# Two attention stages of a two-layer transformer kernel: projection work placed between the head pairs, and query products merged two heads at a time

## What is computed

```python
# layer 0
proj = h @ w_in                      # c_q (256), c_kv (128), k_r (32), qB, kB, vB (512 each)
qA = (_rmsnorm(c_q, g_q) @ w_uq).reshape(B_, S, MLA_HEADS, MLA_QK)     # 8 heads of 64 + 32
q_nope, q_rope = qA[..., :MLA_NOPE], qA[..., MLA_NOPE:]
q_rope = _rope(q_rope, cos[None, :, None, :], sin[None, :, None, :])
kv = (_rmsnorm(c_kv, g_kv) @ w_ukv).reshape(B_, S, MLA_HEADS, MLA_NOPE + MLA_V)
oA = _mla_causal_attention(...)      # softmax over all earlier tokens, 8 heads
oB = _dilated_attention(qB, kB, vB, dil_slopes)   # 8 heads, three dilation patterns
return jnp.concatenate([oA, oB], axis=-1) @ w_out
# layer 1
qkv = h @ w_qkv                      # 16 query heads, 2 key/value heads of 64
return _swa_sink_attention(q, k, v, sinks, swa_slopes) @ w_out
```

## Time and profile before

| what | us |
|---|---|
| median of three runs | 1615.84 |
| the profiled execution, as timed | 1617.18 |
| its span, first to last instruction | 1615.2 |
| PE busy (matmuls) | 1432.0 |
| DVE busy | 682.2 |
| ACT busy | 540.5 |
| layer 0: from the first spread transposes to the end of e_out | 959.0 to 1106.8 |
| layer 1: the same to the end of o_out | 1309.2 to 1411.0 |
| the two feed-forward parts | 1117 to 1305, 1419.5 to the end |

### The profile page before, as it was taken

How to read it: one execution, slowest core, us unless ns; L and a number is a source line. 1 busy time by engine, 2 the same in 40 slices (tenths; PEclk the granted TensorE clock), 3 DMA queues, 4 the chain that set the end, 5 groups by cost and what they waited for, 6 DMA issues and landing times.

```text
span 1615.2 us, 25662 instructions
## 1 busy us (share of the span) xinstructions
PE 1432.0 (89%) x10764; PEld 1149.9 (71%) x10764; DVE 682.2 (42%) x1035; ACT 540.5 (33%) x853; POOL 46.8 (3%) x53
## 2 busy tenths in 40 slices
PE   6999998999779888888898869868999987899997
PEld 6989997878655444444454449557999986689997
DVE  4434786635631101101111044575555547565554
ACT  2453675144320100101001034445334345453333
POOL 0000000400020000000000000000000000000000
PEclk8987999989969999999999989969999998999999
DMA  7531442112348999999999983203545622155520
GB/s 289 186 128 53 163 166 90 55 53 92 142 196 346 428 428 429 428 428 428 428 428 428 429 365 131 79 1 133 201 176 192 226 88 79 61 187 195 181 92 27
DMA packets 27434, 349.54 MB, mean 216 GB/s; under 512 B 3041, under 2 KB 3297, under 8 KB 4578
## 3 DMA queue, kind: packets, MB, share of 16 engines
q1 hardware_dynamic: 27218, 347.46, 53.8%
q10 hardware_dynamic: 144, 1.05, 0.2%
HBM read 347.45 MB, written 1.05 MB: 216 GB/s over the span
## 4 chain that ended last, share of the span: by engine, by line
PE 69%; DMA 15%; DVE 9%; ACT 4%; issue 2%; SPq 1%; POOL 0%; DVEq 0%; POOLq 0%; ACTq 0%
PE psum L410 67%; DMA ring<-in_w 14%; ACT pages L1055 2%; DVE slot_lo L1587 2%; PE psum L479 1%; DVE pages L2068 1%; DVE pages L1722 1%; ACT mix_hi L1084 1%; DVE pages L2100 1%; DVE pages L2072 0%; DMA ab<-in_w_ab 0%; DVE pages L1548 0%; PE psum L763 0%; ACT pages L1310 0%; DVE pages L2155 0%
## 5 line engine op out<-in xcount | busy, mean ns | idle before, releaser
L410 PE MATMUL psum<-ring,pages 128*64 128x256 f32 (+1 forms) x2564 | 359.7, 438 | 67.4 <-DMA ring<-in_w 48.7
L410 PEld LDWEIGHTS psum<-ring,pages 128*64 128x64 f32 x2564 | 186.5, 142 | 225.6 <-issue 80.2
L410 PE MATMUL psum<-x_hi,gu_hi 128*128 128x256 f32 x704 | 199.9, 284 | 3.4 <-DVE x_lo L1574 3.4
L410 PE MATMUL psum<-x_hi,gu_lo 128*128 128x256 f32 x704 | 199.9, 284 | 0.0
L410 PE MATMUL psum<-x_lo,gu_hi 128*128 128x256 f32 x704 | 199.9, 284 | 0.0
L410 PE MATMUL psum<-pages 64*64 64x64 f32 (+10 forms) x1760 | 145.6, 275 | 20.4 <-ACT pages L1055 10.2
L410 PE MATMUL psum<-h_hi,mix_hi 128*128 128x256 f32 x512 | 149.0, 291 | 1.1 <-DVE slot_lo L1587 1.1
L410 PEld LDWEIGHTS psum<-pages 64*64 64x64 f32 (+4 forms) x1760 | 115.3, 161 | 48.4 <-issue 24.1
L410 PE MATMUL psum<-h_lo,mix_hi 128*128 128x256 f32 x512 | 147.3, 288 | 0.0
L410 PE MATMUL psum<-h_hi,slot_lo 128*128 128x256 f32 x512 | 147.2, 287 | 0.0
L1587 DVE TENSOR_TENSOR slot_lo<-ring,mix_hi 128x2048 fp32r<-128x2048 f32 x44 | 101.8, 2317 | 101.5 <-ACT mix_hi L1084 101.2
(11 more groups left out here) (222 smaller groups left out, 2154.0 us busy)
## 6 DMA issues: line engine op xcount, KB each, us to landing
ring<-in_w SPq DMA_DIRECT2D x96, 2048.0 KB, 18.1
ring<-in_ffn SPq DMA_DIRECT2D x44, 1536.0 KB, 6.5
ring<-in_w_in SPq DMA_DIRECT2D x16, 2048.0 KB, 8.1
ring<-in_e_in SPq DMA_DIRECT2D x3, 2048.0 KB, 14.4
ring<-in_w_pa SPq DMA_DIRECT2D x2, 2048.0 KB, 8.1
ring<-in_w_pb SPq DMA_DIRECT2D x2, 2048.0 KB, 8.7
ring<-in_w_o SPq DMA_DIRECT2D x2, 2048.0 KB, 7.7
ring<-in_e_out SPq DMA_DIRECT2D x2, 2048.0 KB, 15.0
```

What stands on the lines that cost most here:

```text
L410: return pe.matmul(o, lhsT, rhs, start=start, stop=stop, skip_group_check=True)
```

## The change

The two sections of layer 0 become one run of `attend` over eight pairs of heads (four mla, then four dil). `attend` now calls a function `fill(i)` on PE behind the scores of pair i+1, and a function `between(i)` on ACT (behind the exponentials of pair i) and on DVE (at the end of step i). Those hold half units of projections and their cutting. In layer 0 the units qB1, kB1, vB0, vB1 (half in each of steps 0 to 7) and the first half item of e_out (steps 8 and 9) move into `attend`; qB0 and kB0 stay ahead of it. vB is now made in units like the others. In layer 1 the key and value projection comes first, then unit qS0; qS1 stands whole in step 0, qS2 in steps 1 and 2, qS3 in steps 3 and 4, and the first half item of o_out in steps 8 and 9. Scores use banks 0 and 1 only, fills banks 2 and 3. Scores and values issue the two heads of a pair alternately. Weight columns of each head's latent query are laid out as 64 + 32 + 32 swapped, so that one product of 128 columns makes all of them and two heads share a bank: 16 logical matmuls in place of 32, and half as many, twice as wide instructions on ACT and DVE behind them. The ring item o_kv is loaded ahead of o_in.

```diff
-            def attend(sec, nheads, operands, values):
...
+            def attend(heads, fill, scores_need, values_need):
+
+                def scores(j):
+                    sec, n, operands, _ = heads[j]
+                    if j in scores_need:
+                        pe.wait_ge(*V(*scores_need[j]))
+                    o = [take(f"{sec}s{2 * n + h2}", h2) for h2 in range(2)]
+                    for qs, width in ((slice(0, P), P), (slice(P, T), T)):
+                        for h2 in range(2):
...
                 scores(0)
+                for i in range(len(heads) + 2):
+                    if i + 1 < len(heads):
                         scores(i + 1)
+                    fill(i)
                     if i >= 2:
...
-            for hd in range(HEADS):
-                name = f"qA{hd}"
+            for n in range(HEADS // 2):
+                name = f"qA{n}"
                 o = take(name)
-                for k in range(2):
-                    mm(o[0:NOPE + ROPE, 0:T], wq[:, k, hd * 96:(hd + 1) * 96], cq[:, k, :], k == 0, k == 1)
...
+                for half in range(2):
+                    for k in range(2):
+                        hd = 2 * n + half
+                        last = mm(o[:, half * T:(half + 1) * T], wq[:, k, hd * P:(hd + 1) * P], cq[:, k, :], k == 0, k == 1)
...
+            def late_fill(i):
+
+                if i == 0:
+                    split_unit("qS1", ("o_in", 0), 1, page_high[3], x, bank=2)
+                elif i < 3:
+                    split_unit("qS2", ("o_in", 1), 0, page_high[4], x, (i - 1,), 3)
+                elif i < 5:
+                    split_unit("qS3", ("o_in", 1), 1, page_high[3], x, (i - 3,), 2)
+                elif i >= 8:
+                    tokens_half("o_out", 0, ("o_out", 0), 0, page_high[4], y, split_ready(4), blocks=(i - 8,), banks=(2, 3))
+
             pe.wait_ge(*V("kvS_ready", 2))
+            attend(heads, late_fill, {2 * n: ("qS_ready", n + 1) for n in range(4)}, {})
...
+            def late_between(i):
+
+                if i == 0:
+                    split_high(MIXER_PAIRS + 16)
+                    queries_out(1)
+                elif i == 1:
+                    split_high(MIXER_PAIRS + 17)
+                elif i == 3:
+                    queries_out(2)
+                    split_high(MIXER_PAIRS + 18)
+                elif i == 5:
+                    queries_out(3)
+                    split_high(MIXER_PAIRS + 19)
+                elif i in (6, 7):
+                    input_high(page_part[9], fm(12), late, blocks=(i - 6,))
...
+            def late_lows(i):
+
+                for at, upto in ((0, 16), (1, 17), (3, 18), (5, 19)):
+                    if i == at:
+                        split_low(MIXER_PAIRS + upto)
```

More of the change, by code:

```diff
@@ L420, in project_split @@
                     for pair in range(2):
[L421 to L432, removed]
@@ new lines, in project_tokens, with value_unit @@
+                        tokens_half(part, i, item, c, highs[c], x, ready, width)
+            def value_unit(name, item, c, high, x, blocks, bank):
+                if 0 in blocks:
+                    split_chunk(item, c, high, (name,))
+                    take(name, bank)
+                o = bank_of(name)
+                w = {"hi": high.rearrange("p (k c) -> p k c", c=256), "lo": chunk_of(slot_low[slot_no(item_no[item])], c)}
+                for b in blocks:
+                    for k in range(KD):
+                        for n, (wp, xp) in enumerate(PARTS):
+                            last = mm(o[:, b * T:(b + 1) * T], x[xp][:, k, b * P:(b + 1) * P], w[wp][:, k, :],
+                                      k == 0 and n == 0, k == KD - 1 and n == 2)
+                if 1 in blocks:
+                    give(last, name)
+                    if c:
+                        release(item, name)
@@ L866, in attend @@
                         pe.wait_ge(*V(f"{sec}_pT", n + 1))
[L867 to L874 removed]
+                        o = take(f"{sec}o{n}", 6 + j % 2)
@@ new lines, in _, with early_fill @@
+            dil = (lambda i: (qB[half_of(i), i // 2, :], kB[half_of(i), i // 2, :]), lambda g, b: vB[:, b, g * VDIM:(g + 1) * VDIM])
+            heads = [("mla", n) + mla for n in range(HEADS // 2)] + [("dil", n) + dil for n in range(HEADS // 2)]
+            y = {"hi": page_part[3], "lo": page_part[2]}
+            def early_fill(i):
+                if i < 2:
+                    split_unit("qB1", ("e_in", 1), 1, page_high[11], x, (i % 2,), 2)
+                elif i < 4:
+                    split_unit("kB1", ("e_in", 2), 1, page_high[12], x, (i % 2,), 3)
+                elif i < 6:
+                    value_unit("vB0", ("e_in", 3), 0, page_high[11], x, (i % 2,), 2)
+                elif i < 8:
+                    value_unit("vB1", ("e_in", 3), 1, page_high[12], x, (i % 2,), 3)
+                else:
+                    tokens_half("e_out", 0, ("e_out", 0), 0, page_high[11], y, split_ready(3), blocks=(i % 2,), banks=(2, 3))
@@ L2101, in attend @@
                                                 ALU.mult), f"{sec}_probs" if b else None)
-                for n in range(pairs - 2, pairs):
-                    output(sec, n)
+                    between(i)
+                for j in range(len(heads) - 2, len(heads)):
+                    output(*heads[j][0:2])
             def output(sec, n):
```

390 lines of the change are left out of this document (218 added, 172 removed).

## The result

The changed kernel takes 1605.82 us (median of 13; 1598.59 to 1609.37 without one disturbed run) against 1615.84: ratio 0.9931, 95% interval 0.9917 to 0.9945. Its profiled execution took 1604.6 (span 1602.8, clock 0.949). The forecast was 1604.5.

The account below looks back on a forecast made before the run. Attention was taken as bound by DVE's 4.1 us per pair and the chain across engines, with PE idle beside it. Layer 0 -22.2, layer 1 +1.2 and clock +9.6 sum to -11.4: 1604.5 us against 1615.8, range 1592 to 1613.

Parts of the forecast that it names:

- Ahead of layer 0's attention: Projections before layer 0's attention: units moved away 22.7 and latent products 9.6, less 0.8, make 31.5 us less; start at 999.8.
- Layer 0's attention: Layer 0's merged attention: 51 us of PE work plus 16 us of waits, 67.0; layer 0 gains 22.2 at full clock.
- Layer 1: Layer 1: attention takes 67.6 us instead of 42.2, o_out ends at 1412.2 instead of 1411.0, a loss of 1.2.
- the sources of the waits: Layer 0's attention: 16 us from two score banks, DVE's cuts waiting for ACT's copy, and the last steps (2 us).
- the two banks: Layer 0's attention: scores of the next pair wait until DVE empties the same two banks; before there were four.
- The clock: Both attentions: half clock behind eight waits of 2.5 to 4.1 us costs 1.2 us each, 9.6 in all.
- clock holds: Rival for both attentions: dense fills keep full clock, -21.0 us and up to 2 more, 1594; chance 0.17.
- Small items: Head alternation, mode switches and DMA: alternation could bring 2 us, switches move the sum under 2, DMA 0 to 2.
- changed feed-forward parts: Sign of error, outside the mixers: the prediction is wrong if the feed-forward parts change; no size given.
- full cover: Rival: fill covers all waits and PE is the bound, attentions of 51 and 45.5 us, total 1557; chance 0.03.
- Half clock right through: Rival for both layers: half clock stays, PE blocks 1.3 times as long, +7 us together, 1623; chance 0.10.
- the slower rope: Rival in layer 0's latent queries: DVE's rope takes 2.5 per pair instead of 2.1, 1.6 us lost; no separate chance.

Follow-up runs that it names:

- experiment 7: Changed kernel with useless identity matmuls put into PE's longest waits in both attentions: 1599.89 us, ratio 0.9914.
- experiment 1: Changed kernel with layer 1 put back (all query units ahead of attention, no fill, scores over four banks), layer 0 as changed: 1593.34 us, ratio 0.9865.
- experiments 3 to 6: Changed kernel with helpers moved: 3 two query evacuations (1595.83 us); 4 ACT's and DVE's (1569.62); 5 only DVE's (1591.91); 6 as 4, layer 0 only ACT's (1573.28).
- 9: Kernel before the change with one edit, scores on banks 0 and 1 only instead of four: 1611.78 us, ratio 0.9981.
- the reordered kernel: Changed kernel with ACT's and DVE's cuts and evacuations placed elsewhere in both layers, PE untouched: 1569.62 us, ratio 0.9705; run again 1567.92 us, 0.9721.
- experiment 10: The changed kernel itself, unedited, profiled and run once more: 1607.98 us (1595.51 to 1610.22).
- with more fill: Kernel with ACT's and DVE's helpers reordered, plus output projection half items earlier and more of them in layer 1's attention: 1563.62 us, ratio 0.9686.
- experiment 8: Changed kernel with the two heads of a pair issued one behind the other in scores and values, not alternately: 1602.56 us, ratio 0.9928.

## Why the prediction was right, step by step

The mechanism was right: an interleaved attention bound by the order of helpers on ACT and DVE, a gain in layer 0 and a loss in layer 1. That the total came within 1.3 us is in part luck. The two mixers were to bring -11.4 us and brought -8.6; stages that the prediction left alone brought another -3.8, of which -4.3 is no effect of the change.

- **Ahead of layer 0's attention**: 40.8 us forecast, 41.6 measured. The latent products took 14.1 us (forecast 13, before 22.6), and DVE's rope on two heads three operations of 0.68 or 0.69 each, 2.17 per pair from start to start (forecast 2.1, rival 2.5; one head in the earlier trace rows). Window, then DVE's timeline:
```profile
976.50:990.60 14.10, 12.95 (x54) 8.93 (x55) 13.01 (x17) 7.39 (x11) 0.00 (x0) 1.00 0.00 1
```
```profile
981.85 0.69 DVE L2312 SCALAR_TENSOR_TENSOR pages<-psum,pages 32x512 f32<-32x512 f32 x1
```
- **Layer 0's attention**: 67.0 at full clock; experiment 7 had 67.5 and experiment 1 68.4, both at 0.95. The four waits of 4.1, 2.8, 2.9 and 3.0 were measured as 3.58, 2.84, 3.02 and 3.58, at the named places. With the clock the stretch took 74.8, above the stated 67 to 74.
- **Layer 1**: the two waits for evacuated queries of 4.1 were 3.91 and 3.90; those of 1.9 and 4.0 ahead of scores 2 and 3 were 1.70 and 3.94; the 2.5 ahead of scores 7 was 1.31, so there were seven waits over 2.5 us and not eight. The stretch 67.6 at full clock was 67.9 in experiment 7 (0.95); o_out's rest 18.0 (forecast 17.8). The loss was +4.7, forecast 1.2 plus half of the clock's 9.6, 6.0.
- **Of the sources of the waits**, the order of ACT and DVE is shown (experiments 3 to 6); the two banks, which the prediction listed first, cost nothing by themselves (9). There they were tested beside two cuts per attention and no fill; but in the reordered kernel, with all cuts and fills and also on two banks, no wait for them was over 1.17 us.
- **The clock**: 9.6 forecast. The two attentions took 7.8 and 2.8 us more than the walk at full clock, 10.6 together, but not evenly split as the 4.8 and 4.8 of the sum were. The price per wait was mis-sized both ways, and it is no constant: with the same code and waits layer 0 lost only 1.4 over the walk in experiment 1. The 1.2 was also low by the prediction's own rows, since the transposes behind the 4.06 took 1.54 instead of 0.87, 0.7 us on top of the 1.5. The rival "clock holds" (1594) was near in some executions: the changed kernel's runs reach down to 1598.6, and to 1595.5 in experiment 10.
- **Small items**: the prediction counts two more mode switches for each half unit between scores and values. By the row shapes, scores of 64 rows (64*128) and values (128*64) differed already, so a fill of 128*128 adds one, and none in mla, whose scores have 96 rows. No run isolates its price.
- **Not forecast**: unchanged stages moved by -3.8 together. The first block ends between 952 and 959 us in the profiles of all kernels here, whatever the change, so -4.3 is no effect of it. ffn1's +1.9 seems to be one: from the end of o_out to the end of the kernel it is 205.8 to 206.4 us in all ten profiles with layer 1's fill, and 204.3 to 205.5 in the four without. Why the clock falls there is not shown. Windows of the first 5 us of ffn1, before and after:
```profile
1419.46:1424.46 5.00, 5.00 (x42) 5.00 (x43) 2.81 (x2) 3.09 (x3) 0.00 (x0) 1.00 0.01 3
```
```profile
1405.57:1410.57 5.00, 5.00 (x29) 5.00 (x30) 2.96 (x2) 2.94 (x3) 0.00 (x0) 0.66 0.02 3
```
  PE is busy in both, but the second is partly at half clock: 29 matmuls against 42. The prediction named changed feed-forward parts as a sign of error; this 0.1% it had missed.
- **The rivals**: full cover (1557) had 0.03 and is false for this order, yet it is near what the work allows: attentions of 52.9 and 50.3 us, 1563.6 in all, were reached by the order of the same work alone. The walk would have told so, had I moved the helpers in it. Half clock right through (1623) and the slower rope fell.

## What to carry to other kernels

Work put into another stage's idle time brings its helpers along: here the cuts and evacuations on ACT and DVE, not PE, decided whether 17 us of hidden projections in layer 1 were a gain (its mixer -11.8 with the helpers early, -18.9 with more fill) or a loss (+4.7). On an in-order engine put a helper whose inputs are ready ahead of what waits for another engine, not behind it. A hand-made walk of three engines with durations from one profile got the stretches within 2.3 us where the clock in the attention was at 0.94 or more, and missed by up to 9 (92.8 against 84.0) where it was not; use it to try orders, not only to price the one given.

## What the runs showed of the hardware

- A stretch of the same 426 matmuls with four waits of about 3 us took from 68.4 to 75.1 us, with the granted clock at 0.95 and 0.84; with three of the waits filled (experiment 7) it stood at 0.95, with all of them gone (4, layer 0) at 1.00. In two executions of the reordered kernel layer 1's attention had 0.94 and 0.91: behind the same wait of 1.17 us the clock stood at 1.00 in the first (30 matmuls in 3.4 us) and at 0.50 in the second (17). The Trainium skill, page TensorE: Matmul & The Clock Gate, section What's actually happening, says of the start of a kernel that the number of matmuls at the low clock differs between runs of one kernel; here it differs in the middle of one too.
- Alternating two heads' values between the halves of the output rows takes 12 matmuls from 1.14 to 0.88 us (experiment 8). The Trainium skill, page TensorEngine Tiling (Array Packing), section Key Properties, has tiles work in parallel; the row agrees.
- A DVE operation on 32 partitions costs 0.42 us for 256 columns and 0.69 for 512, so two heads at once save a fifth.
